# A mixture-of-experts stage: down projection in three reduced passes over split operands, and its weights' order in the queue

## The chip, the cores and the metric

One core of one Trainium2 chip runs the whole program. The metric is the device time in microseconds of one execution; all runs here are on one core.

## The reference

Two transformer stacks are computed one after the other on 256 tokens of 1024 features. The layer that matters here is the feed-forward part of the second layer of the first stack, a mixture of eight experts with two choices for each token:

```python
def moe_swiglu(h, router_w, w1, w3, w2):
    top_v, top_i = lax.top_k(h @ router_w, TOP_K)          # TOP_K = 2, N_EXPERTS = 8
    probs = jax.nn.softmax(top_v, axis=-1)
    gates = jnp.sum(jax.nn.one_hot(top_i, N_EXPERTS) * probs[..., None], axis=-2)
    out = jnp.zeros_like(h)
    for e in range(N_EXPERTS):
        out = out + gates[..., e:e + 1] * swiglu(h, w1[e], w3[e], w2[e])
    return out                                             # swiglu: (silu(h @ w1) * (h @ w3)) @ w2
```

w1 and w3 are 1024x1408 for each expert, w2 is 1408x1024, all in float32. The rest (a hybrid mixer, two more stacks of attention with short convolutions, four more dense feed-forward parts, modulation from a condition) is not touched by the change.

## The kernel before

Matrix products are made in three passes nearly everywhere. A weight `w` is split into a high part, which ScalarE writes as a copy in the reduced 32-bit type F32R, and a low part, the difference, which VectorE writes in the same type. The activations are split likewise, and TensorE adds high times high, low times high and high times low in one PSUM bank. The splits of all weights go through one ring `WS` of three slots: ScalarE may write unit n as soon as TensorE has finished unit n - 3 (`unit_done`, `unit_done >= n - 2`), VectorE follows it (`split_high`), and TensorE follows VectorE (`split_both`).

The expert phase (`experts()` on each engine, `load_experts()` on SyncE) works on 11 blocks of 128 slots. A slot holds one token for one expert, and `BLOCK_EXPERT` says which expert's weights a block needs, so SyncE reads that number and asks for the weights block by block. For each block:

- **up**: 16 units (`UP_UNITS`), two for each of eight k-tiles of 128 rows: even units are w1 rows, odd ones w3 rows, 1408 columns. Raw rows come as k-tiles (w1 and w3 rows together, 2 x 704 KB) into `RAW`, three slots. A unit is nine passes (columns 512, 512, 384). In blocks 0 to 6 small products with `w_ada_2` (`ada_rows`, `ada_turned`) stand between units 1, 6 and 11, and ScalarE asks for the next 1.57 MB of `w_ada_2` when it comes to unit 11 (blocks 0 to 5).
- **turn**: ScalarE takes the silu, VectorE multiplies (three pieces, L2134), TensorE turns the hidden activations in three pieces (L935), ScalarE copies them to `HIDT` (L1583). Between the first and the second piece TensorE scatters the output of the block before to its tokens (L949), and VectorE later adds that to the residual (eight operations, L1956).
- **down**: 11 k-tiles (`GT`) of w2, two products of 128x512 each, on whole float32 operands: raw w2 rows come as pairs of k-tiles (1024 KB, the sixth half as much) into `W2R`, four slots, and TensorE reads them there (L959). In even blocks, behind the sixth k-tile, TensorE gathers the tokens of the next two blocks (`gather`, L879) and their gates (`slot_gates`, L887); VectorE has made the selecting matrices before (`pick`, L2034 and L2035), ScalarE copies the gathered tokens (`block_high`, L1542) and the gates (L1549), and VectorE makes the low parts (`block_low`, L2057). The gather needs the banks of the scatter, so it waits until all eight residual additions are done.
- **output**: ScalarE scales and copies two halves to `YS` (L1598), VectorE makes the low part (L2154) and, ahead of that, the scattering matrix (`place`, L2043 and L2044). The up pass of the next block may run its unit 0 (w1) at once, but unit 1 needs the banks that hold the output, so it waits for `moe_y_split`.

All weights of the phase are asked for on one queue in program order, so a request that waits for its slot holds all behind it. The order for block b is k-tile 0, the last two pairs of block b - 1, k-tiles 1 and 2, pairs 0 and 1, k-tile 3, pair 2, k-tiles 4 and 5, pair 3, k-tiles 6 and 7. A k-tile waits until the k-tile three before it is split; a pair waits until TensorE has multiplied the pair four before it.

## Time and profile before

| | us |
|---|---|
| median of 3 runs | 3255.27 (3250.29 to 3255.81) |
| the profiled execution | 3252.38 |
| its span, first to last instruction | 3250.6 |
| TensorE busy (matmul records) | 3044.6, 94% of the span |
| VectorE busy | 1504.8, 46% |
| ScalarE busy | 1264.3, 39% |
| mean granted TensorE clock | 0.962 of full speed |
| first up unit of block 0 to the end of down of block 10 | 704 to 1362, about a fifth of the span |

A matmul record can overlap the next, so busy TensorE is not TensorE at its peak; the chain of waits shows what released each instruction. A period in this text is the time from the end of the up pass of one block to the end of the up pass of the next; it is even or odd by the block at which it starts. There are ten, from 742.15 to 1340.06.

### The profile page before, as it was taken

The numbers are of one execution on the slowest core, as the hardware profiler recorded it, in microseconds if no ns is written. First come the engines' busy times: TensorE is split into PE (matmuls) and PEld (weight loads), VectorE is DVE, ScalarE is ACT, GpSimd is POOL, SyncE is SP. The second block draws the span as 40 slices with busy tenths as digits, with TensorE's granted clock in tenths as the row PEclk, the third lists the DMA queues.
The fourth block names the chain that finished last, engine by engine and source line by source line (L and its number), as shares of the span: only waits on it lengthen the run. The fifth ranks groups of instructions, "written<-read, shape, count | busy, mean of one in ns | idle before, by whom it ended". The sixth has DMA issues, their size and how long they took to land.

```text
span 3250.6 us, 43934 instructions
## 1 busy us (share of the span) xinstructions
PE 3044.6 (94%) x16943; PEld 2449.5 (75%) x16943; DVE 1504.8 (46%) x2172; ACT 1264.3 (39%) x1789; POOL 0.2 (0%) x4
## 2 busy tenths in 40 slices
PE   6998998989999999789999999999999999989899
PEld 5887887976676666567777777777787777777898
DVE  4553446556566555542323455433334233356555
ACT  4453334444444444342222344432224222245444
POOL 0000000000000000000000000000000000000000
PEclk8999999979999999889999999999999999999899
DMA  8738773367887876636364121443534636422454
GB/s 292 248 114 254 212 241 119 103 232 279 337 338 270 320 300 262 218 112 200 91 173 141 56 85 28 115 149 85 144 102 119 201 96 169 145 69 75 136 168 133
DMA packets 493957, 563.29 MB, mean 173 GB/s; under 512 B 14979, under 2 KB 449734, under 8 KB 493638
## 3 DMA queue, kind: packets, MB, share of 16 engines
q1 hardware_dynamic: 414278, 442.46, 41.2%
q10 hardware_dynamic: 79488, 118.12, 11.4%
q8 instruction: 140, 2.29, 0.3%
q14 instruction: 51, 0.42, 0.0%
HBM read 559.48 MB, written 1.05 MB: 172 GB/s over the span
## 4 chain that ended last, share of the span: by engine, by line
PE 81%; ACT 6%; DMA 6%; DVE 5%; issue 2%; SPq 0%; ACTq 0%; DVEq 0%
PE bank L709 19%; PE bank L711 18%; PE bank L710 18%; PE bank L959 6%; DMA weights_raw<-in_moe_w 4%; PE bank L737 3%; PE bank L908 2%; PE bank L910 2%; PE bank L909 2%; ACT ring L1457 2%; DMA ada_halves<-in_ada_w 1%; DVE weights_split L2048 1%; PE bank L744 1%; PE bank L1355 1%; ACT weights_split L1534 1%
## 5 line engine op out<-in xcount | busy, mean ns | idle before, releaser
L709 PE MATMUL bank<-hn_split,weights_split 128*128 128x256 f32 (+1 forms) x2480 | 875.1, 353 | 68.7 <-DVE hn_split L1938 28.8
L711 PE MATMUL bank<-hn_split,weights_split 128*128 128x256 f32 (+1 forms) x2480 | 849.9, 343 | 2.0 <-issue 2.0
L710 PE MATMUL bank<-hn_split,weights_split 128*128 128x256 f32 (+1 forms) x2480 | 850.5, 343 | 0.0
L1892 DVE TENSOR_TENSOR weights_split<-weights_raw,weights_split 128x1024 fp32r<-128x1024 f32 (+1 forms) x430 | 553.9, 1289 | 248.7 <-ACT weights_split L1403 245.4
L1403 ACT ACTIVATE weights_split<-weights_raw 128x1024 fp32r<-128x1024 f32 (+1 forms) x430 | 475.3, 1107 | 454.6 <-PE bank L711 443.8
L709 PEld LDWEIGHTS bank<-hn_split,weights_split 128*128 128x128 f32 x2480 | 483.7, 195 | 203.3 <-issue 113.1
L711 PEld LDWEIGHTS bank<-hn_split,weights_split 128*128 128x128 f32 x2480 | 483.2, 195 | 52.2
L710 PEld LDWEIGHTS bank<-hn_split,weights_split 128*128 128x128 f32 x2480 | 484.4, 195 | 49.7 <-issue 1.9
L1975 DVE TENSOR_TENSOR ring<-ring,bank 128x512 f32<-128x512 f32 (+1 forms) x110 | 63.9, 581 | 705.7 <-PE bank L711 649.3
L2048 DVE TENSOR_TENSOR weights_split<-weights_raw,weights_split 128x1408 fp32r<-128x1408 f32 x176 | 282.7, 1623 | 180.8 <-ACT weights_split L1534 180.8
L1534 ACT ACTIVATE weights_split<-weights_raw 128x1408 fp32r<-128x1408 f32 x176 | 239.2, 1381 | 194.8 <-DMA weights_raw<-in_moe_w 122.0
L709 PE MATMUL bank<-hidden_split,weights_split 128*128 128x512 f32 (+1 forms) x880 | 308.6, 351 | 0.0
L710 PE MATMUL bank<-hidden_split,weights_split 128*128 128x512 f32 (+1 forms) x880 | 305.1, 347 | 0.0
L711 PE MATMUL bank<-hidden_split,weights_split 128*128 128x512 f32 (+1 forms) x880 | 305.1, 347 | 0.0
L908 PE MATMUL bank<-weights_split,block_split 128*128 128x512 f32 x528 | 210.4, 398 | 23.3 <-DVE weights_split L2048 23.2
L1492 ACT ACTIVATE hidden_split<-ring 128x512 fp32r<-128x512 f32 (+1 forms) x110 | 60.1, 546 | 420.7 <-DVE ring L1975 420.7
L959 PE MATMUL bank<-expert_down,block_hidden_turned 128*128 128x512 f32 x484 | 210.8, 593 | 0.0
L910 PE MATMUL bank<-weights_split,block_split 128*128 128x512 f32 x528 | 201.3, 381 | 0.0
L909 PE MATMUL bank<-weights_split,block_split 128*128 128x512 f32 x528 | 200.0, 379 | 0.0
L709 PEld LDWEIGHTS bank<-hidden_split,weights_split 128*128 128x128 f32 x880 | 166.6, 189 | 32.4 <-issue 11.3
L711 PEld LDWEIGHTS bank<-hidden_split,weights_split 128*128 128x128 f32 x880 | 166.7, 189 | 20.9
L710 PEld LDWEIGHTS bank<-hidden_split,weights_split 128*128 128x128 f32 x880 | 166.7, 189 | 19.8
(362 smaller groups left out, 2964.6 us busy)
## 6 DMA issues: line engine op xcount, KB each, us to landing
weights_raw<-in_moe_w SPq DMA_DIRECT2D x176, 704.0 KB, 7.5
weights_raw<-in_w_ffn_in SPq DMA_DIRECT2D x176, 512.0 KB, 5.1
ada_halves<-in_w_ada ACTq DMA_DIRECT2D x96, 768.0 KB, 5.2
expert_down<-in_moe_w SPq DMA_DIRECT2D x55, 1024.0 KB, 8.9
ada_halves<-in_ada_w ACTq DMA_DIRECT2D x54, 768.0 KB, 4.9
weights_raw<-in_w_in SPq DMA_DIRECT2D x60, 512.0 KB, 4.8
weights_raw<-in_w_ffn_out SPq DMA_DIRECT2D x32, 768.0 KB, 4.7
weights_raw<-in_ffn_w SPq DMA_DIRECT2D x44, 512.0 KB, 5.4
```

Of the source, the lines that this page charges most:

```text
L709: mm(ps, wh, xh, start=first, stop=False)
L710: mm(ps, wh, xl, start=False, stop=False)
L711: return mm(ps, wl, xh, start=False, stop=last)
L737: i = mm(PS[bank][32 * j:32 * j + 32, 0:ADA_COLS], condp[:, 4 * h + j, :], AH[:, h, j, :], start=h == 0, stop=h == 1)
L908: mm(ps, xh, wh, start=k == 0, stop=False)
L909: mm(ps, xl, wh, start=False, stop=False)
L910: i = mm(ps, xh, wl, start=False, stop=k == KT - 1)
L959: i = mm(PS[4 + h][:, :], HIDT[:, f, :], W2R[:, m % W2_PAIRS, f % 2, h * 512:(h + 1) * 512], start=f == 0, stop=f == GT - 1)
L1403: act.activation(split_view(slot, 0, kts, n), raw, ACT.Copy).then_inc(split_high, 1)
L1534: act.activation(up_split(n, 0), up_raw(n), ACT.Copy).then_inc(split_high, 1)
L1892: tt(split_view(slot, 1, kts, n), raw, split_view(slot, 0, kts, n).bitcast(F32), ALU.subtract)\
L2048: tt(up_split(n, 1), up_raw(n), up_split(n, 0).bitcast(F32), ALU.subtract).then_inc(split_both, 1)
```

## The change

The down projection is made in three passes like the others. w2's k-tiles become units 16 to 26 of each block in the ring of splits (`BLOCK_UNITS` = 27), so ScalarE and VectorE split them as they do the up units. `HIDT` gets a high and a low part, the low one made by VectorE (`hidden_low`) from the bank that ScalarE copied. The six passes of a k-tile replace two whole products. `W2R` has three slots in place of four, and a pair waits until the pair three before it is split. SyncE's order for block b becomes: k-tiles 0, 1 and 2, then pairs 3, 4 and 5 of block b - 1, then k-tile 3, pair 0, k-tile 4, pair 1, k-tile 5, pair 2, k-tiles 6 and 7. The programs of ScalarE and VectorE in `experts()` are reordered: the splits of w2's later k-tiles stand among VectorE's residual additions, ScalarE's copies of the gather stand behind the copy of unit 23, and the splits of units 0 and 1 of the next block stand ahead of the placing and the output, that of unit 2 behind them. The wait for all splits at the end of `load_experts` now includes w2's. The diff, without lines that only rename or count semaphores:

```diff
+BLOCK_UNITS = UP_UNITS + GT
 UP_CHUNKS = ((0, 512), (512, 512), (1024, 384))
-W2_PAIRS = 4
+W2_PAIRS = 3
...
-        HIDT, _ = at("block_hidden_turned", FFN_GROUP, [P, GT, P], F32, g_at + W2_PAIRS * 2 * D + FFN_GROUP)
+        HIDT, _ = at("block_hidden_turned", 2 * FFN_GROUP, [P, 2, GT, P], F32R, g_at + W2_PAIRS * 2 * D + FFN_GROUP)
...
                     kk = KT * b + k
-                    sp.wait_ge(split_both, MOE_U + 2 * max(0, kk - 2))
+                    sp.wait_ge(split_both, MOE_U + ((kk - 3) // KT * BLOCK_UNITS + 2 * ((kk - 3) % KT) + 2 if kk >= 3 else 0))
...
                         m = n - W2_PAIRS
-                        sp.wait_ge(S["moe_down"], GT * (m // DOWN_PAIRS) + min(2 * (m % DOWN_PAIRS) + 2, GT))
+                        sp.wait_ge(split_both, MOE_U + m // DOWN_PAIRS * BLOCK_UNITS + UP_UNITS + min(2 * (m % DOWN_PAIRS) + 2, GT))
...
                     expert[b] = sp.value_load(BLOCK_EXPERT[0:1, b:b + 1], min_val=0, max_val=EXPERTS - 1)
-                    up_tile(b, 0)
+                    for k in range(3):
+                        up_tile(b, k)
                     if b:
-                        down_pair(b - 1, 4)
-                        down_pair(b - 1, 5)
-                    up_tile(b, 1)
-                    up_tile(b, 2)
-                    down_pair(b, 0)
-                    down_pair(b, 1)
-                    up_tile(b, 3)
-                    down_pair(b, 2)
-                    up_tile(b, 4)
-                    up_tile(b, 5)
-                    down_pair(b, 3)
+                        for q in range(3, DOWN_PAIRS):
+                            down_pair(b - 1, q)
+                    for k in range(3, 6):
+                        up_tile(b, k)
+                        down_pair(b, k - 3)
                     up_tile(b, 6)
                     up_tile(b, 7)
-                down_pair(MOE_BLOCKS - 1, 4)
-                down_pair(MOE_BLOCKS - 1, 5)
-                sp.wait_ge(split_both, MOE_U + UP_UNITS * MOE_BLOCKS)
+                for q in range(3, DOWN_PAIRS):
+                    down_pair(MOE_BLOCKS - 1, q)
+                sp.wait_ge(split_both, MOE_U + BLOCK_UNITS * MOE_BLOCKS)
...
 
                 def down(b):
                     for f in range(GT):
-                        pe.wait_ge(S["moe_hidden_copied"], 3 * b + f // 4 + 1)
-                        m = DOWN_PAIRS * b + f // 2
-                        pe.wait_ge(wide_full[m % W2_PAIRS], 16 * (m // W2_PAIRS + 2))
+                        n = BLOCK_UNITS * b + UP_UNITS + f
+                        pe.wait_ge(S["moe_hidden_split"], 3 * b + f // 4 + 1)
+                        pe.wait_ge(split_both, MOE_U + n + 1)
+                        hh, hl = (HIDT[:, part, f, :] for part in (0, 1))
                         for h in range(2):
-                            i = mm(PS[4 + h][:, :], HIDT[:, f, :], W2R[:, m % W2_PAIRS, f % 2, h * 512:(h + 1) * 512],
-                                   start=f == 0, stop=f == GT - 1)
+                            wh, wl = (expert_split(n, part)[:, h * 512:(h + 1) * 512] for part in (0, 1))
+                            mm(PS[4 + h][:, :], hh, wh, start=f == 0, stop=False)
+                            mm(PS[4 + h][:, :], hl, wh, start=False, stop=False)
+                            i = mm(PS[4 + h][:, :], hh, wl, start=False, stop=f == GT - 1)
                             if h:
-                                i.then_inc(S["moe_down"], 1)
+                                i.then_inc(unit_done, 1)
...
-                def split_up(n):
-                    block = MOE_B + n // 2
-                    act.wait_ge(raw_full[block % 3], 32 * (block // 3 + 1))
+                def split_expert(n):
+                    b, v = n // BLOCK_UNITS, n % BLOCK_UNITS
+                    if v < UP_UNITS:
+                        block = MOE_B + KT * b + v // 2
+                        act.wait_ge(raw_full[block % 3], 32 * (block // 3 + 1))
+                    else:
+                        m = DOWN_PAIRS * b + (v - UP_UNITS) // 2
+                        act.wait_ge(wide_full[m % W2_PAIRS], 16 * (m // W2_PAIRS + 2))
                     act.wait_ge(unit_done, MOE_U + n - 2)
-                    act.activation(up_split(n, 0), up_raw(n), ACT.Copy).then_inc(split_high, 1)
+                    act.activation(expert_split(n, 0), expert_raw(n), ACT.Copy).then_inc(split_high, 1)
...
                 table(ACT.Silu)
                 block_high(0, 1)
                 for n in range(3):
-                    split_up(n)
+                    split_expert(n)
                 slot_gates(0, 1)
+                last = BLOCK_UNITS * MOE_BLOCKS
                 for b in range(MOE_BLOCKS):
-                    for v in range(3, UP_UNITS):
+                    n = BLOCK_UNITS * b
+                    for v in range(3, UP_UNITS + 1):
                         if v == 11 and b + 1 < x.n_turns:
                             copy_ada(b + 1)
-                        split_up(UP_UNITS * b + v)
-                    act.wait_ge(unit_done, MOE_U + UP_UNITS * b + UP_UNITS - 1)
+                        split_expert(n + v)
+                    act.wait_ge(unit_done, MOE_U + n + UP_UNITS - 1)
                     for c, (c0, cn) in enumerate(UP_CHUNKS):
                         act.activation(HID[:, c0:c0 + cn], PS[c][:, 0:cn], ACT.Silu).then_inc(S["moe_silu"], 1)
+                    split_expert(n + UP_UNITS + 1)
                     for c, (c0, cn) in enumerate(UP_CHUNKS):
                         act.wait_ge(S["moe_hidden_turned"], 3 * b + c + 1)
-                        act.activation(HIDT[:, 4 * c:4 * c + cn // P, :].rearrange("p a b -> p (a b)"),
+                        act.activation(HIDT[:, 0, 4 * c:4 * c + cn // P, :].rearrange("p a b -> p (a b)"),
                                        PS[7 if c == 1 else 6][:, 0:cn], ACT.Copy).then_inc(S["moe_hidden_copied"], 1)
-                    if b + 1 < MOE_BLOCKS:
-                        split_up(UP_UNITS * (b + 1))
-                    if b + 1 < MOE_BLOCKS:
-                        if b % 2 == 0:
+                        if c == 0:
+                            split_expert(n + UP_UNITS + 2)
+                    for v in range(UP_UNITS + 3, BLOCK_UNITS + 1):
+                        if n + v < last:
+                            split_expert(n + v)
+                        if v == UP_UNITS + 7 and b % 2 == 0 and b + 1 < MOE_BLOCKS:
                             block_high(b + 1, 2)
                             slot_gates(b + 1, 2)
-                        split_up(UP_UNITS * (b + 1) + 1)
-                        split_up(UP_UNITS * (b + 1) + 2)
+                    if b + 1 < MOE_BLOCKS:
+                        split_expert(n + BLOCK_UNITS + 1)
                     act.wait_ge(S["moe_gate_copied"], (b + 1) // 2 + 1)
                     if b:
                         act.wait_ge(S["moe_scattered"], 4 * b)
                     for h in range(2):
-                        act.wait_ge(*((S["moe_down"], GT * (b + 1)) if h else (S["moe_y_part"], b + 1)))
+                        act.wait_ge(*((unit_done, MOE_U + BLOCK_UNITS * (b + 1)) if h else (S["moe_y_part"], b + 1)))
                         act.activation(YS[:, 0, h * 512:(h + 1) * 512], PS[4 + h][:, :], ACT.Copy,
                                        scale=SLOT_GATE[:, b % 4:b % 4 + 1]).then_inc(S["moe_y_high"], 1)
+                    if b + 1 < MOE_BLOCKS:
+                        split_expert(n + BLOCK_UNITS + 2)
                 u0 = next_split[0] = PH["ffna.0"][0]
...
+                def split_expert(n):
                     dve.wait_ge(split_high, MOE_U + n + 1)
-                    tt(up_split(n, 1), up_raw(n), up_split(n, 0).bitcast(F32), ALU.subtract).then_inc(split_both, 1)
+                    tt(expert_split(n, 1), expert_raw(n), expert_split(n, 0).bitcast(F32), ALU.subtract).then_inc(split_both, 1)
+
+                def hidden_low(b, c):
+                    dve.wait_ge(S["moe_hidden_copied"], 3 * b + c + 1)
+                    cn = UP_CHUNKS[c][1]
+                    hh, hl = (HIDT[:, part, 4 * c:4 * c + cn // P, :].rearrange("p a b -> p (a b)") for part in (0, 1))
+                    tt(hl, PS[7 if c == 1 else 6][:, 0:cn], hh.bitcast(F32), ALU.subtract).then_inc(S["moe_hidden_split"], 1)
...
 
                 for b in range(MOE_BLOCKS):
-                    for v in range(3, UP_UNITS):
-                        split_up(UP_UNITS * b + v)
+                    n = BLOCK_UNITS * b
+                    for v in range(3, UP_UNITS + 1):
+                        split_expert(n + v)
                     if b + 1 < x.n_turns:
                         add_modulation(b + 1)
                     for c, (c0, cn) in enumerate(UP_CHUNKS):
                         dve.wait_ge(S["moe_silu"], 3 * b + c + 1)
-                        dve.wait_ge(*((S["moe_up_part"], 2 * b + c + 1) if c < 2 else (unit_done, MOE_U + UP_UNITS * (b + 1))))
+                        dve.wait_ge(*((S["moe_up_part"], 2 * b + c + 1) if c < 2 else (unit_done, MOE_U + n + UP_UNITS)))
                         tt(HID[:, c0:c0 + cn], HID[:, c0:c0 + cn], PS[3 + c][:, 0:cn], ALU.mult).then_inc(S["moe_hidden"], 1)
+                    split_expert(n + UP_UNITS + 1)
+                    hidden_low(b, 0)
+                    split_expert(n + UP_UNITS + 2)
+                    hidden_low(b, 1)
+                    hidden_low(b, 2)
                     if b + 1 < MOE_BLOCKS and b % 2 == 0:
                         pick(b + 1, 0, 2)
                         pick(b + 2, 1, 2)
-                    if b:
-                        for k in range(KT):
-                            dve.wait_ge(S["moe_scattered"], 4 * (b - 1) + k // 2 + 1)
-                            residual(k, 0, PS[(2, 3, 0, 1)[k // 2]][:, k % 2 * SEQ:(k % 2 + 1) * SEQ], gate(k),
+                    for v in range(UP_UNITS + 3, BLOCK_UNITS):
+                        split_expert(n + v)
+                        q = v - UP_UNITS - 3
+                        for k in (2 * q, 2 * q + 1) if b and q < 4 else ():
+                            dve.wait_ge(S["moe_scattered"], 4 * (b - 1) + q + 1)
+                            residual(k, 0, PS[(2, 3, 0, 1)[q]][:, k % 2 * SEQ:(k % 2 + 1) * SEQ], gate(k),
                                      x0 + KT * (b - 2) + k + 1 if b > 1 else None)
                     if b + 1 < MOE_BLOCKS:
-                        split_up(UP_UNITS * (b + 1))
                         if b % 2 == 0:
                             block_low(b + 1, 2)
-                        split_up(UP_UNITS * (b + 1) + 1)
-                        split_up(UP_UNITS * (b + 1) + 2)
+                        split_expert(n + BLOCK_UNITS)
+                        split_expert(n + BLOCK_UNITS + 1)
                     place(b)
                     dve.wait_ge(S["moe_gate_copied"], (b + 1) // 2 + 1)
                     for h in range(2):
...
                             ALU.mult, ALU.subtract).then_inc(S["moe_y_split"], 1)
+                    if b + 1 < MOE_BLOCKS:
+                        split_expert(n + BLOCK_UNITS + 2)
                 u0 = next_split[0] = PH["ffna.0"][0]
```

## Rows read from the trace of the kernel before

**Rows 1.** The page's costliest groups, down's matmuls: busy us, mean ns.

```profile
L959 PE MATMUL bank<-expert_down,block_hidden_turned 128*128 128x512 f32 x484 | 210.8, 593 | 0.0
```

**Rows 2.** Windows, even periods summed, then odd: length, busy, PEclk, DMA share, GB/s.

```profile
sum 306.50, PE 297.54 PEld 215.00 DVE 186.62 ACT 143.76 POOL 0.00; mean PE 59.51 PEld 43.00 DVE 37.32 ACT 28.75 POOL 0.00
...
1161.81:1219.95 58.14, 55.03 (x217) 38.73 (x214) 32.57 (x32) 25.94 (x24) 0.00 (x0) 0.97 0.74 298
1281.41:1340.06 58.65, 54.35 (x217) 38.63 (x215) 32.86 (x32) 26.05 (x24) 0.00 (x0) 0.97 0.68 271
sum 291.41, PE 278.09 PEld 194.98 DVE 164.59 ACT 131.12 POOL 0.00; mean PE 55.62 PEld 39.00 DVE 32.92 ACT 26.22 POOL 0.00
```

**Rows 3.** Chain of waits in two periods: start us, us, what.

```profile
1164.93 18.89 PE bank L959 x44
1183.81 0.23 PE bank L908
...
1233.56 3.83 PE bank L879 x32
...
1246.88 0.23 PE bank L908
```

**Rows 4.** Timeline of ScalarE: start us, us, engine, line, operation, idle before it.

```profile
974.54 2.65 ACT L1534 ACTIVATE weights_split<-weights_raw 128x1408 fp32r<-128x1408 f32 x2 [2.02 <-DMA weights_raw<-in_moe_w]
...
1187.75 1.38 ACT L1534 ACTIVATE weights_split<-weights_raw 128x1408 fp32r<-128x1408 f32 x1 [0.54 <-PE bank L910]
1189.67 1.38 ACT L1534 ACTIVATE weights_split<-weights_raw 128x1408 fp32r<-128x1408 f32 x1 [0.53 <-PE bank L910]
...
1207.37 2.65 ACT L1534 ACTIVATE weights_split<-weights_raw 128x1408 fp32r<-128x1408 f32 x2 [3.23 <-DMA weights_raw<-in_moe_w]
1210.83 1.38 ACT L1534 ACTIVATE weights_split<-weights_raw 128x1408 fp32r<-128x1408 f32 x1 [0.82 <-DMA weights_raw<-in_moe_w]
```

**Rows 5.** Timeline of TensorE, the first pass of unit 12.

```profile
1210.46 0.50 PE L908 MATMUL bank<-weights_split,block_split 128*128 128x512 f32 x1 [1.78 <-DVE weights_split L2048]
```

**Rows 6.** Windows of one period, columns as in rows 2.

```profile
1157.00:1169.00 12.00, 12.00 (x60) 9.02 (x60) 9.04 (x15) 6.11 (x9) 0.00 (x0) 1.00 0.01 2
...
1175.00:1211.00 36.00, 32.89 (x131) 23.83 (x130) 20.50 (x16) 17.77 (x15) 0.00 (x0) 1.00 1.02 414
1211.00:1214.00 3.00, 3.00 (x9) 2.58 (x8) 2.57 (x2) 1.21 (x1) 0.00 (x0) 0.50 0.59 242
```

**Rows 7.** Timeline of SyncE's queue, down's fifth and sixth pair asked for.

```profile
930.07 3.77 SPq L649 DMA_DIRECT2D expert_down<-in_moe_w  x2
...
1168.53 3.77 SPq L649 DMA_DIRECT2D expert_down<-in_moe_w  x2
```

**Rows 8.** Timeline of all engines, the first two splits after the expert phase.

```profile
1362.84 2.00 ACT L1403 ACTIVATE weights_split<-weights_raw 128x1024 fp32r<-128x1024 f32 x2
...
1363.92 2.36 DVE L1892 TENSOR_TENSOR weights_split<-weights_raw,weights_split 128x1024 fp32r<-128x1024 f32 x2 [0.19 <-ACT weights_split L1403]
```

**Rows 9.** Timeline of VectorE, odd period.

```profile
1160.69 1.85 DVE L2134 TENSOR_TENSOR block_hidden<-block_hidden,bank 128x512 f32<-128x512 f32 x3 [1.50 <-PE bank L910]
...
1183.87 1.46 DVE L2154 SCALAR_TENSOR_TENSOR block_out_split<-bank,small,block_out_split 128x512 fp32r<-128x512 f32 x2 [1.02 <-ACT block_out_split L1598]
```

**Rows 10.** Timeline of VectorE, even period.

```profile
1220.86 0.28 DVE L2034 TENSOR_SCALAR block_pick<-route_tables,small 128x128 fp32r<-128x128 f32 x1
...
1223.19 3.22 DVE L1956 SCALAR_TENSOR_TENSOR residual<-bank,mod_first,residual 128x256 f32<-128x256 f32 x8
...
1236.21 1.42 DVE L2057 TENSOR_TENSOR block_split<-bank,block_split 128x256 fp32r<-128x256 f32 x4 [8.27 <-ACT block_split L1542]
```

**Rows 11.** Timeline of ScalarE, even period, the last copy of the gates.

```profile
1238.51 0.27 ACT L1549 ACTIVATE small<-bank 128x1 f32<-128x1 f32 x2
```

**Rows 12.** The tile of w_ada, two loads of two halves each.

```profile
DMA to landing us min/median/max: 12.5/14.2/16.5
```

**Rows 13.** Timeline of VectorE after the last block, its first residual.

```profile
1366.20 0.87 DVE L1956 SCALAR_TENSOR_TENSOR residual<-bank,mod_first,residual 128x256 f32<-128x256 f32 x2
```

32 lines of the change are left out of this document (17 added, 15 removed).

## The prediction

> **What bounds the kernel now.** I first read the page, to see what the diff touches: the matmuls of down, 484 records for 242 instructions, are 210.8 us of TensorE, all in the expert phase [rows 1]. So I cut that phase into periods, each from the end of one block's up pass to the end of the next one's. The ten periods fall into two kinds [rows 2]: five that start at an even block take 306.5 us (61.3 each), five that start at an odd one 291.4 us (58.3 each). In the even ones TensorE also gathers the tokens of the next two blocks. The reader should see in the sums that VectorE is busy for only 186.6 and 164.6 us of them, so its total is no limit.
>
> The chain of waits shows what a period is made of [rows 3]. Below, t counts from the end of the up pass. Odd: turning and scattering until 3.1, 44 records of down for 18.89 us, next up pass from 1183.81, t = 22.0. Even: the same with the gather (3.83) and the gates in between, next up pass from 1246.88, t = 26.9. An up unit takes 1.92 us [rows 4], so 16 take 30.7; the pass that starts at 1183.81 ends at 1219.95, after 36.1. The 5.4 us too many are transfers: ScalarE stands waiting for k-tiles 6 and 7 of w1 and w3 [rows 4]. k-tile 6 lands at 1207.37, unit 12 starts at 1210.46 after 1.78 us of idle TensorE [rows 5], 3.09 later (one split on each engine), and four units more would end the pass at 1218.1. The other 1.8 us are the clock: the granted clock reads 0.50, the lower of the two levels, from 1211 to 1214 [rows 6].
>
> Why are the tiles late? From 1157 to 1169 nothing moves (2 GB/s), from 1175 on 414 GB/s for 36 us [rows 6]. The queue is in order, and it stands at the fifth pair of w2, which waits for the second k-tile of down; it is issued at 1168.53 [rows 7]. So the period is idle queue, then a burst, then four last units.
>
> **The change, part by part.** *TensorE.* A pass over 512 columns takes 512/1408 of a third of 1.92 us, 0.232; six of them make a k-tile of down 1.39 us, eleven 15.3, where 44 matmuls of the old kind take 18.89. Unhidden, this would give 3.6 us a block.
>
> *The splits.* Per block eleven copies on ScalarE and eleven subtractions on VectorE, 128x1024: two in a row take 2.00 and 2.36 us [rows 8], so 1.0 and 1.15 us each. VectorE gets 12.7 us a block, and 1.75 more for the low half of the activations (no row shows this operation; 1408 columns of a PSUM product take 1.85 [rows 9], four of 256 columns 1.42 [rows 10]; I take the rate of the first, the second would give 1.95). Both total busy times stay far under the period. But they fall into the down stage, behind one another in program order, so I lay out that stage.
>
> *Odd block.* VectorE ends the last hidden product at t = 0.73 (1162.54) [rows 9], splits k-tile f1 until 1.9, halves the first third of the activations until 2.55, f2 until 3.7, the other thirds until 4.85. TensorE starts f0 at 3.1 as before. Slots of the split ring come free only three units later, so f3's copy waits for f0 (4.5): its split ends at 6.85. Now two residual additions (0.40 each, eight in 3.22 us [rows 10]) follow each of f3 to f6: splits end at 6.85, 8.85, 10.8, 12.75, then 14.7, 15.85, 17.0 and 18.5 for f10. TensorE follows them and ends down at 20.3, where before it was 22.0: 1.7 of the 3.6 us are left. Then come the splits of up units 0 and 1 (1.54 each in a row) until 22.2, the placing (0.75, estimated from two operations of 256 columns) and the halving of the output (1.46 [rows 9]) until 24.4. Before, the placing and both splits lay earlier, in idle time. Unit 1 needs the output's banks, so it starts at 24.45, against 22.0 + 1.92 = 23.9.
>
> *Even block.* The eight pick operations (1220.86 until the first residual at 1223.19, 2.4 us with the overlap [rows 10]) come ahead of f3. Splits then end at 8.4, 10.35, 12.3 and 14.25, the last residual at 15.05. The gather waits for all residuals, so it starts at 15.05 although f5 ends at 13.8. ScalarE's copy for f8 stands behind the copies of the gather in its program; those end 5.2 us after the gather starts (1233.56 to 1238.78 [rows 3, 11]), at 20.3. So f8's split ends at 22.5, f9's 23.65, f10's 24.8; then block_low (twice 1.42) until 27.6, unit 0's split 29.15, unit 1's 30.7, placing and output until 32.95. Up starts at 29.2 and its unit 1 at 33.0; before 26.9 and 28.85. Block 0 has no residuals: 28.0 in place of 30.7.
>
> *The queue.* The k-tiles 0 to 2 of the next block are now asked for as units 11, 13 and 15 are split, and the last pairs as down is split. All of that lands within the first 14 us. But k-tile 3 still waits for the split of unit 1, R = 22.2 (odd), 30.7 (even), 28.0 (block 0), and the first pair of w2 stands behind it. The idle stretch is not gone, it has moved, and more must come after it: five k-tiles of 2 x 704 KB and three pairs of 1024 KB, 10.4 MB (the shapes in the code). At 414 GB/s [rows 6], with 1.5 us of start that I estimate from the time between the issue at 1168.53 and the rise to that rate (bounds 0 and 4), k-tile 6 lands at R + 23.0, k-tile 7 at R + 26.5. By the 3.05 us of two splits and four units this ends the pass at R + 33.75. From unit 1 on TensorE alone would end at R + 2.25 + 28.8 = R + 31.05, so transfers stay last.
>
> In the up passes of blocks 1 to 5, 1.57 MB of w_ada are loaded too, from about R + 17. They took 14.2 us to land [rows 12], about 0.27 of the rate: up to 3.3 us for k-tile 7; the kernel before needs 44.5 us from the first request to that tile with them (930.07 to 974.54 [rows 7, 4]) and 42.3 without (1168.53 to 1210.83): 2.2. I take 2.5, so k-tile 7 lands at R + 29.0 and the pass ends at R + 35.9. (The Trainium skill, "DMA: Bandwidth & Descriptors", section "Queues, rings and completion order", has each DMA engine go round its queues packet by packet, which would give w_ada up to half of the engines. Its whole 1.57 MB would then be ahead of k-tile 7, 3.8 us for 2.5, and five such periods would make the sum 6.5 us higher; the 14.2 us of the row speak for a smaller share.)
>
> *Ends.* In the first up pass one pair less is ahead of k-tile 7 (1 MB, 2.5 us at 414 GB/s), and the queue stands idle once more, since k-tile 3 must wait for unit 1's split and no second pair fills that time: 0, with 2.5 us of gain as the bound. After the last block down ends 1.7 us earlier, but ffna's first weights are now asked for after the last split (t = 18.6; before, right behind the last pair), land near 23.5 (1 MB, for which I estimate 5 us with the start), and both engines split two units of them before the residuals (2.00 and 2.36 us, the second 1.2 us behind the first): these start near 27.0, before at 1366.20 - 1340.06 = 26.1 [rows 2, 13]. +0.9.
>
> *Sum.* Even periods: 63.9 + 2 x 66.6 + 2 x 64.45 = 326.0 against 306.5, +19.5. Odd: 2 x 58.1 + 3 x 55.95 = 284.05 against 291.4, -7.4. With +0.9: +13.0. The span becomes 3263.6. The profiled execution took 3252.4 for a span of 3250.6 and the median of the runs is 3255.3, so I add the 13 to that: 3268 us.
>
> **Rivals.** *1. Transfers no longer bind (faster).* If k-tile 6 lands before R + 20.3, TensorE's own time holds: odd 53.25, even 61.8 (block 0: 59.1), and 1.9 more (one unit, an estimate) where w_ada is multiplied in. That makes 270.1 and 312.0 us, with the end -15: 3240 us. For it: three k-tiles are ready early. Against: 8.9 MB after R at 414 GB/s. It decides at some 475 GB/s, which no window that I read reaches. A cheaper way to the same side: vector splits that run ahead so that the even handover costs 3 us less in five periods, -15: 3253. Chance of ending below -0.2%: 0.2.
>
> *2. The splits and the moved requests cancel.* Each even period 2 to 4 us shorter than laid out, because a wait that I put in series overlaps: 3250 to 3261 us. 0.2.
>
> *3. As forecast*, 3262 to 3275 us: 0.4.
>
> *4. The clock also falls.* Now the periods from 1161.81 and 1281.41 read 0.97 [rows 2], as do two others of the ten. The new down stage has TensorE idle for about 0.5 to 1 us ahead of most k-tiles and 2.5 us ahead of the even up pass. One fall costs 1.8 us where nothing covers it; in all ten periods 18: 3286 us. 0.2. (The Trainium skill, "TensorE: Matmul & The Clock Gate", section "HAM oscillation", describes just this, a clock that falls again at each wait for a transfer; the trace so far shows it in under half of the periods.)
>
> Range: rival 1 below, rival 4 above, 3238 to 3290. A difference under 0.2% (6.5 us) can't be told from none here. Chances from the cases: faster 0.2, same 0.2, slower 0.6; the likeliest case alone 3262 to 3275.
>
> **What would show it.** Right: down stages of about 20.3 us to its end in odd blocks, 26.7 in even; up starting at 20.7 and 29.2; a wait before up unit 1 on the output's halving; the queue empty from t = 14 to R; ScalarE waiting for k-tiles 5 to 7; even periods longer by 3 to 5 us and odd ones shorter by 1 to 2. Wrong: no wait for transfers in up (rival 1), even handovers below 27 us (rival 2), or a clock of 0.97 in most periods (rival 4). What would upset the whole is a VectorE whose splits take another time than 1.15 us, since the even handover adds some sixteen of its operations in series.

## The result and the profile after

| | before | after |
|---|---|---|
| median, us (5 runs each) | 3252.2 (3247.06 to 3255.81) | 3288.87 (3286.66 to 3293.43) |
| ratio | | 1.0111, interval 1.0099 to 1.0123 |
| span of the profiled execution | 3250.6 | 3284.9 |
| mean granted clock | 0.962 | 0.962 |

The change makes the kernel 36.7 us slower, where 13 were forecast. The page of the kernel after, busy time and the chain's shares by engine and by line:

```profile
PE 3023.5 (92%) x17185; PEld 2489.5 (76%) x17185; DVE 1659.6 (51%) x2326; ACT 1388.8 (42%) x1910; POOL 0.2 (0%) x4
...
PE 75%; DVE 10%; ACT 7%; DMA 6%; issue 3%; SPq 1%; ACTq 0%; DVEq 0%
PE bank L709 19%; PE bank L711 18%; PE bank L710 18%; DVE weights_split L2063 4%; DMA weights_raw<-in_moe_w 4%; PE bank L737 3%; PE bank L908 2%; PE bank L910 2%; PE bank L909 2%; ACT weights_split L1542 2%; ACT ring L1460 1%; DMA ada_halves<-in_ada_w 1%; DVE residual L1971 1%; PE bank L744 1%; PE bank L1358 1%
```

VectorE has 155 us more work and is still at 51% of the span; TensorE has 21 us less. Nothing here says slower. The periods do. Windows over the even ones (the first and the last of five), then over the odd ones (the fourth of five), each with its sum (columns as in [rows 2]):

```profile
740.05:807.03 66.98, 59.06 (x285) 47.56 (x284) 49.04 (x55) 40.15 (x47) 0.00 (x0) 0.95 0.74 290
...
1251.93:1318.42 66.49, 56.17 (x279) 45.94 (x277) 51.66 (x62) 39.67 (x46) 0.00 (x0) 1.00 0.69 260
sum 337.85, PE 295.50 PEld 239.59 DVE 256.37 ACT 199.94 POOL 0.00; mean PE 59.10 PEld 47.92 DVE 51.27 ACT 39.99 POOL 0.00
...
1193.48:1251.93 58.45, 52.90 (x239) 42.35 (x237) 46.91 (x46) 37.24 (x36) 0.00 (x0) 0.97 0.77 298
...
sum 298.96, PE 269.78 PEld 213.83 DVE 235.25 ACT 187.62 POOL 0.00; mean PE 53.96 PEld 42.77 DVE 47.05 ACT 37.52 POOL 0.00
```

Against the sums of [rows 2] the even periods are 31.35 us longer and the odd ones 7.55, together 38.9. The prediction had 19.5 and -7.4. The rest of the 34.3 us between the spans: the first period starts 2.1 us earlier (740.05 for 742.15), since its up pass began 3.2 us earlier, at 701.80 for 704.97, and took 1.2 us longer; the first residual behind the last block comes at 1406.40, t = 29.5, for 26.1 [rows 2, 13], so +3.4; and from there to the end, in code that the change doesn't touch, this execution took 5.9 us less (1878.5 for 1884.4).

**The handover.** The chain of waits in the odd period from 1193.48 and the even one from 1251.93 (start us, us, what), where [rows 3] had one unbroken down:

```profile
1198.27 1.07 ACT weights_split L1542
...
1204.34 0.87 DVE residual L1971 x2
1205.21 1.13 DVE weights_split L2063
1206.35 0.79 DVE residual L1971 x2
1207.13 1.14 DVE weights_split L2063
...
1212.93 3.16 DVE weights_split L2063 x2
1216.10 0.28 DVE first_choice_place L2058
1216.43 0.37 issue
1216.80 1.41 DVE block_out_split L2182 x2
1218.25 0.50 PE bank L908
...
1265.98 0.80 DVE residual L1971 x2
1266.83 4.10 PE bank L879 x32
...
1277.01 2.65 DVE block_split L2078 x8
1279.66 3.07 DVE weights_split L2063 x2
1282.73 0.28 DVE first_choice_place L2058
1283.06 0.37 issue
1283.43 1.41 DVE block_out_split L2182 x2
1284.89 0.51 PE bank L908
```

VectorE's program order is the chain from the third k-tile of down to the next block's unit 1. By t: R, the end of unit 1's split, is 22.6 (1216.09), unit 1 at 24.8 (1218.25); in the even period the gather starts at 14.9, R is 30.8 (1282.73), unit 1 is at 33.0. The forecast was 22.2, 24.45, 15.05, 30.7, 33.0.

**The up pass.** ScalarE's timeline, in which it waits for k-tiles 4 to 7 in turn (k-tile 7 is the line of the single split), and SyncE's queue, which asks for k-tile 3 right after R:

```profile
1229.07 2.65 ACT L1542 ACTIVATE weights_split<-weights_raw 128x1408 fp32r<-128x1408 f32 x2 [1.39 <-DMA weights_raw<-in_moe_w]
1235.07 2.65 ACT L1542 ACTIVATE weights_split<-weights_raw 128x1408 fp32r<-128x1408 f32 x2 [3.35 <-DMA weights_raw<-in_moe_w]
1241.06 2.65 ACT L1542 ACTIVATE weights_split<-weights_raw 128x1408 fp32r<-128x1408 f32 x2 [3.34 <-DMA weights_raw<-in_moe_w]
1244.52 1.38 ACT L1542 ACTIVATE weights_split<-weights_raw 128x1408 fp32r<-128x1408 f32 x1 [0.81 <-DMA weights_raw<-in_moe_w]
```

```profile
1195.67 9.26 SPq L654 DMA_DIRECT2D expert_down<-in_moe_w  x3
1216.25 0.35 SPq L644 DMA_DIRECT2D weights_raw<-in_moe_w  x1
```

k-tile 6 lands at R + 25.0 and k-tile 7 at R + 28.4, where 23.0 and 26.5 were forecast, and the pass ends at R + 35.8 for 33.75. Windows of the same stretch (last column GB/s) show the start of the burst in halves of a microsecond, then its steady rate:

```profile
1216.50:1217.00 0.50, 0.35 (x2) 0.03 (x1) 0.50 (x2) 0.23 (x2) 0.00 (x0) 1.00 0.00 0
1217.00:1217.50 0.50, 0.00 (x0) 0.00 (x0) 0.50 (x2) 0.50 (x1) 0.00 (x0) 1.00 0.69 123
1217.50:1218.00 0.50, 0.00 (x0) 0.00 (x0) 0.50 (x2) 0.50 (x1) 0.00 (x0) 1.00 0.81 203
1218.00:1218.50 0.50, 0.25 (x1) 0.25 (x2) 0.50 (x2) 0.32 (x1) 0.00 (x0) 1.00 0.70 248
1218.50:1219.00 0.50, 0.50 (x3) 0.41 (x3) 0.50 (x1) 0.00 (x0) 0.00 (x0) 1.00 1.02 406
...
1219.00:1237.00 18.00, 17.05 (x79) 14.11 (x78) 12.45 (x9) 10.12 (x8) 0.00 (x0) 1.00 1.02 414
```

The rate is the 414 GB/s of [rows 6]. 10.36 MB at that rate are 25.0 us; k-tile 7 took 28.4. So 3.4 us come on top, not 1.5. A window from R to the landing of k-tile 7 shows where the rest is:

```profile
1216.09:1244.50 28.41, 24.55 (x106) 19.96 (x105) 20.00 (x17) 15.45 (x12) 0.00 (x0) 0.94 0.97 389
```

389 GB/s over 28.41 us are 11.05 MB, 0.69 more than the tiles up to k-tile 7 hold. So about 1.7 us are lost before the rate is up, and another 1.7 lie between the last bytes of k-tile 7 and the landing that ScalarE sees, in which bytes of later requests move already.

**The clock.** The last 8 us of the up passes of blocks 4, 6, 7 and 8, in windows (the clock is the third number from the end):

```profile
989.69:997.69 8.00, 8.00 (x32) 6.79 (x31) 5.56 (x7) 5.54 (x7) 0.00 (x0) 0.80 1.03 403
1119.30:1127.30 8.00, 8.00 (x33) 6.86 (x31) 5.66 (x7) 4.59 (x7) 0.00 (x0) 0.80 0.79 277
1185.48:1193.48 8.00, 7.77 (x36) 6.67 (x37) 7.10 (x7) 5.55 (x7) 0.00 (x0) 1.00 0.97 357
1243.93:1251.93 8.00, 7.78 (x37) 6.68 (x37) 7.09 (x7) 5.55 (x7) 0.00 (x0) 1.00 0.92 335
```

The passes of blocks 1 to 6 all read 0.80 to 0.87 there, those of 7 to 10 all 1.00 (that of block 0, with w_ada's products too, also 1.00). From k-tile 6's landing to the end of the pass the six take 12.42 us and the four 10.87. In the kernel before, a pass with the products of `ada_rows` takes 11.68 at full clock. So of those 1.55 us about 0.8 are the products and 0.7 the clock. The kernel before had four such falls (0.84 to 0.89). Three were in passes without these products, blocks 8 to 10, where the same stretch took 12.2 to 12.6 us, and 10.87 is the time at full clock: 1.3 to 1.7 us each. So the clock took no less from the kernel before than from the one after. In block 8 the clock falls too (0.77 from 1237 to 1240, 0.66 to 1243), but earlier, mostly under the wait for k-tile 6.

### The profile page after: what moved, and what is told of

It is laid out like the page before. It is cut to its first block, busy times and chain, and to the rows that moved or that the text cites. A ratio compares the mean times of both kernels' runs of the same rounds, so it can differ in the third digit from the quotient of the medians.

```text
span 3284.9 us, 44814 instructions
## 1 busy us (share of the span) xinstructions
PE 3023.5 (92%) x17185; PEld 2489.5 (76%) x17185; DVE 1659.6 (51%) x2326; ACT 1388.8 (42%) x1910; POOL 0.2 (0%) x4
## 4 chain that ended last, share of the span: by engine, by line
PE 75%; DVE 10%; ACT 7%; DMA 6%; issue 3%; SPq 1%; ACTq 0%; DVEq 0%
PE bank L709 19%; PE bank L711 18%; PE bank L710 18%; DVE weights_split L2063 4%; DMA weights_raw<-in_moe_w 4%; PE bank L737 3%; PE bank L908 2%; PE bank L910 2%; PE bank L909 2%; ACT weights_split L1542 2%; ACT ring L1460 1%; DMA ada_halves<-in_ada_w 1%; DVE residual L1971 1%; PE bank L744 1%; PE bank L1358 1%
## 5 line engine op out<-in xcount | busy, mean ns | idle before, releaser
L908 PE MATMUL bank<-weights_split,block_split 128*128 128x512 f32 x528 | 213.0, 403 | 54.5 <-DVE weights_split L2063 44.6
L910 PE MATMUL bank<-weights_split,block_split 128*128 128x512 f32 x528 | 205.4, 389 | 0.0
L909 PE MATMUL bank<-weights_split,block_split 128*128 128x512 f32 x528 | 204.5, 387 | 0.0
L1492 ACT ACTIVATE ring<-bank 128x512 f32<-128x512 f32 (+1 forms) x110 | 56.3, 512 | 314.3 <-PE bank L711 314.2
```

The lines of the kernel that those rows point to most:

```text
L908: mm(ps, xh, wh, start=k == 0, stop=False)
L909: mm(ps, xl, wh, start=False, stop=False)
L910: i = mm(ps, xh, wl, start=False, stop=k == KT - 1)
```

## Experiments

Below, "up" is the time from the first up unit to the end of the pass, "hand" from the end of the pass to the next first unit. Hand and up, read from each trace's TensorE timeline, are (even / odd, block 0's left out; for up, first the passes of blocks 7 to 10, then those of blocks 1 to 6, which hold w_ada's products). The last column is the time from the end of the first up pass to that of the last:

In the old down the first matmul record of an up pass starts some 0.5 us before down's last product has ended, so its hand is short by that. The start of unit 1 is the same thing in both kernels: it comes 2.32 us after the pass's first record in the old down and 3.55 in the new one (2.76 in e7, e9 and e10).

| kernel | ratio to before, interval | hand | up | all ten periods |
|---|---|---|---|---|
| before | 1 | 26.3 / 21.6 | 34.9 to 37.2, 35.0 to 37.5 | 597.9 |
| after | 1.0111 (1.0099, 1.0123) | 29.4 / 21.2 | 36.8 to 37.2, 39.2 to 40.1 | 636.8 |
| e1 | 1.0012 (1.0003, 1.0022) | 29.4 / 21.2 | 33.2 to 34.7, 35.1 to 36.4 | 600.9 |
| e2 | 0.9981 (0.9970, 0.9992) | 26.3 / 21.6 | 34.4 to 36.7, 34.8 to 36.3 | 594.7 |
| e3 | 1.0064 (1.0044, 1.0084) | 29.4 / 21.2 | 35.7 to 37.7, 35.4 to 39.1 | 624.6 |
| e4 | 0.9995 (0.9982, 1.0009) | 29.4 / 21.2 | 32.8 to 34.8, 35.1 to 36.0 | 597.1 |
| e5 | 0.9898 (0.9875, 0.9921) | 26.3 / 21.6 | 31.1 to 31.5, 33.7 to 33.9 | 566.3 |
| e6 | 0.9943 (0.9922, 0.9964) | 26.3 / 21.6 | 32.5 to 33.7, 34.1 to 35.3 | 580.5 |
| e7 | 0.9960 (0.9944, 0.9975) | 26.4 / 21.4 | 32.8 to 35.4, 34.3 to 35.7 | 582.9 |
| e8 | 0.9946 (0.9930, 0.9962) | 26.7 / 18.8 to 19.9 | 33.3 to 34.6, 35.1 to 38.4 | 583.4 |
| e9 | 0.9907 (0.9890, 0.9924) | 26.4 / 21.4 | 31.6 to 31.7, 34.2 to 34.3 | 570.0 |
| e10 | 0.9922 (0.9905, 0.9938) | 26.4 / 21.4 | 31.6 to 32.2, 34.2 to 34.3 | 570.3 |
| e11 | 0.9896 (0.9880, 0.9913) | 26.3 / 21.6 | 31.4 to 32.5, 33.7 | 569.4 |

### Which half of the change costs: e1, e2, e3

**e1**, after, with the pairs ahead of k-tile 3:

```diff
-                    for k in range(3, 6):
+                    for q in range(3):
+                        down_pair(b, q)
+                    for k in range(3, KT):
                         up_tile(b, k)
-                        down_pair(b, k - 3)
-                    up_tile(b, 6)
-                    up_tile(b, 7)
```

> The changed kernel with one edit: the queue asks for pairs 0, 1 and 2 of a block ahead of its k-tile 3, so that 3.1 MB move while the queue now stands empty (t = 14 to R, where R is the end of unit 1's split). Theory A (the up pass ends when 10.4 MB after R have landed, with 3.4 us of start and landing on top of 414 GB/s, then 3.05 us of splits and two units): only 7.2 MB are left after R, k-tile 7 lands at R + 20.8, before TensorE wants it (R + 24.2), so a period becomes R + 31.05, about 1.9 more with w_ada, 5 us less than now in each of ten: 3289 - 52 = 3237 us. Theory B (the late handover by VectorE and ScalarE sets the pass, and its waits for tiles only mirror it): no change, 3285 to 3293.

Measured: 3256.46 us. The order of the queue alone is worth 32 us of the changed kernel, nearly as much as its whole loss against before, but not the 52 that were expected. Handovers are as in after, to 0.1 us.

**e2**, before, with the next block's k-tiles 0 to 2 asked for first:

```diff
-                    up_tile(b, 0)
+                    for k in range(3):
+                        up_tile(b, k)
                     if b:
                         down_pair(b - 1, 4)
                         down_pair(b - 1, 5)
-                    up_tile(b, 1)
-                    up_tile(b, 2)
```

> The kernel before with only the order of requests changed: k-tiles 0, 1 and 2 of a block ahead of the last two pairs of the block before, then pairs 0 and 1, k-tile 3 and the rest as before; down stays two whole float32 products for each k-tile. Theory A: from the split of unit 1 on (t = 20.2 odd, 23.2 even) 9.3 MB are left, k-tile 7 lands at t = 46.1 and 49.1, the pass would end at 53 and 56, TensorE's own work at 52.7 and 57.6 (1.9 more with w_ada); ten periods 566 in place of 598: 3252 - 32 = 3220 us. Theory B: transfers do not set it, 3245 to 3255.

Measured: 3246.8 us, a gain of 6 us for an expected 32. SyncE's queue and the rates, in one up pass of e2:

```profile
1193.48 0.33 SPq L639 DMA_DIRECT2D weights_raw<-in_moe_w  x1
1193.90 0.38 SPq L640 DMA_DIRECT2D weights_raw<-in_moe_w  x1
1194.47 0.38 SPq L649 DMA_DIRECT2D expert_down<-in_moe_w  x1
1197.32 0.34 SPq L639 DMA_DIRECT2D weights_raw<-in_moe_w  x1
```

```profile
1183.00:1188.00 5.00, 5.00 (x22) 3.76 (x21) 1.60 (x3) 2.76 (x3) 0.00 (x0) 1.00 1.02 421
1188.00:1197.00 9.00, 9.00 (x44) 7.73 (x43) 7.85 (x5) 6.51 (x5) 0.00 (x0) 1.00 0.86 308
```

The requests come 3.84 us apart, as units are split, and the queue runs at 308 GB/s in a stretch where it had room for 414. A k-tile may be asked for only when the one three before it is split, so there is a round from a freed slot to its next contents that the bytes over the rate don't show. That this round was the cause is at this point argued only; e10 and e11 test it.

**e3**, after, with the order of before: k-tile 0, pairs 3 to 5 of the block before, k-tiles 1 and 2, pair 0, k-tile 3, pair 1, k-tiles 4 and 5, pair 2, k-tiles 6 and 7.

> The changed kernel with requests as near to the old order as three slots of w2 allow: k-tile 0, pairs 3 to 5 of the block before, k-tiles 1 and 2, pair 0, k-tile 3, pair 1, k-tiles 4 and 5, pair 2, k-tiles 6 and 7. Theory A: pair 0 has landed before R, so 9.3 MB are left in place of 10.4, k-tile 7 lands 2.5 us earlier in each period: 3264 us. If asking ahead for the k-tiles is what helps the changed kernel (rival), undoing it makes this one slower than 3289. Theory B: no change.

Measured: 3273.64 us, where 3264 were expected. Of the changed kernel's loss 15 us are the new order against the old one (4.8 in the even periods, 7.6 in the odd ones); e1's order is worth 17 more.

### What the new down costs with fewer bytes: e4, e5, e8

**e4** is after and **e5** before, each with a quarter of w3:

```diff
-                    sp.dma_start(RAW[:, s, FFN_GROUP:], a["moe_w3"][0][expert[b]][r, :]).then_inc(raw_full[s], 16)
+                    sp.dma_start(RAW[:, s, FFN_GROUP:FFN_GROUP + 352], a["moe_w3"][0][expert[b]][r, 0:352]).then_inc(raw_full[s], 16)
```

> The changed kernel with only 352 of the 1408 columns of w3 loaded (the rest of the tile keeps what stood there, so part of the up product is left out); order, waits and all work on the engines stay. A k-tile is 0.90 MB in place of 1.44. Theory A: 7.7 MB after R land by R + 21.9, TensorE's own pace holds, period R + 31.05: about 3237 us, as with the pairs first. Theory B: no change, 3285 to 3293.

> The kernel before with only 352 of the 1408 columns of w3 loaded (part of the up product is left out), the partner of the changed kernel with fewer bytes, which took 0.9995 of the kernel before. Here no transfer should bind in either, so the two show what the new down stage costs by itself. Theory A (the handover of the new down stage is longer than the old one: even 29.4 against 26.3 us and unit 1 another 2 us later, odd 21.2 against 21.6 and unit 1 0.5 us later): up passes of 30.7 us (32.8 with w_ada), ten periods 559, 39 us under the kernel before: 3213 us, 37 below its partner. Rival C (three passes are cheaper than whole products as soon as transfers don't bind): this one at or above its partner's 3250.

Measured: 3250.3 us for the 3237 expected, and 3217.77 for 3213. With few bytes the new down still costs 32.5 us. Four even handovers are 3.0 us longer, the first 2.1, five odd ones 0.4 shorter (+12.2); and unit 1 of each block starts 3.55 us after unit 0 in place of 2.32, by the output's low part behind both splits and the placing (+12.3 in ten blocks). The two make 24.4 of the 30.8 us between the ten periods of e4 and e5. The other 6.3 lie between unit 1 and the end of the pass, and are transfers: e4 keeps the changed kernel's order of requests, and ScalarE still waits for k-tiles in it, between 740 and 1309 (us in total, times, longest):

```profile
ACT weights_split L1542 <- DMA weights_raw<-in_moe_w: 22.5, 18, 2.6
```

The same cut fits the full kernels. Of the 38.9 us that the change adds to the ten periods, 24.6 are the later start of unit 1 and the rest the stretch from unit 1 to the end of the pass. e1 leaves the starts of unit 1 where they are in the changed kernel and takes its 36 us from that stretch alone. So its order of requests makes up for the late handover; it doesn't show that the order was the whole cause of the loss.

**e8** is e1 with VectorE's low part made for half of the columns of w2:

```diff
-                    tt(expert_split(n, 1), expert_raw(n), expert_split(n, 0).bitcast(F32), ALU.subtract).then_inc(split_both, 1)
+                    c = slice(0, FFN_GROUP if n % BLOCK_UNITS < UP_UNITS else 512)
+                    tt(expert_split(n, 1)[:, c], expert_raw(n)[:, c], expert_split(n, 0)[:, c].bitcast(F32),
+                       ALU.subtract).then_inc(split_both, 1)
```

> The changed kernel with the pairs first, and VectorE making the low part of only 512 of the 1024 columns of each k-tile of w2 (the other half of the low part is left out). An operation of 1.14 us becomes 0.6. Theory A: odd handovers from 21.2 to about 18.9 us, even ones from 29.4 to about 26.1, 28 us if the tiles are there: 3228 us. If VectorE isn't what sets the down stage, handovers stay at 21.2 and 29.4 and the time at 3256.

Measured: 3232.74 us, 24 less than e1, of which 17.5 lie in the ten periods and the rest behind them; handovers are 2.7 us shorter in even and 1.3 to 2.4 in odd blocks. So VectorE paces the down stage, although it is half idle over the span. It is also why three passes don't shorten the odd handover: it is 21.2 us for 21.6 before, where TensorE's share of it fell by an estimated 3.6.

### Mending the handover and the queue: e6, e7, e9, e10, e11

**e6** is e2 with pairs 2 and 3 both ahead of k-tile 4.

> The old down with the new queue, and pairs 2 and 3 both ahead of k-tile 4. With pair 3 between k-tiles 5 and 6, k-tile 6 took 10.7 us from request to landing, and the transfer engines ran at 265 to 355 GB/s between 1188 and 1197, since each k-tile may be asked for only when the one three before is split. Theory D (three raw slots and what stands between their requests set the up pass): pair 3 fills that dip, k-tiles 6 and 7 land 2.5 us earlier in each of ten periods: 3247 - 25 = 3222 us. Theory E (total bytes at 414 GB/s set it): no change, 3242 to 3252.

Measured: 3233.52 us, faster than both kernels, and about half of the 25 us that theory D gave.

**e7** is e1 with ScalarE's `block_high` behind the copy for f8 (f0 to f10 are down's k-tiles), the residual additions done with f5, the placing behind `hidden_low` (odd) or f7 (even), and `block_low` behind f8:

```diff
-                        if v == UP_UNITS + 7 and b % 2 == 0 and b + 1 < MOE_BLOCKS:
+                        if v == UP_UNITS + 8 and b % 2 == 0 and b + 1 < MOE_BLOCKS:
...
-                        for k in (2 * q, 2 * q + 1) if b and q < 4 else ():
+                        for k in ((0, 1), (2, 3, 4), (5, 6, 7))[q] if b and q < 3 else ():
...
```

> The changed kernel with the pairs first, and three moves in the programs of ScalarE and VectorE: ScalarE's copy for k-tile f8 ahead of the copies of the gather; VectorE's placing in its idle time (odd: ahead of f3; even: behind f7), its residuals done with f5, and block_low behind f8 in place of behind f10. Theory A (the handover is a chain through VectorE's and ScalarE's program order): even handover 29.4 to about 26 us and unit 1 from 33.0 to 29.0, odd unit 1 0.75 us earlier; 24 us in all if the tiles are there: 3256 - 24 = 3232 us. Rival (the slots of raw tiles take it back, since the requests then come no faster in up): 3245 to 3256.

Measured: 3237.76 us, 18.7 less than e1. The even handover is back at 26.4, and unit 1 comes 2.76 us after unit 0, not 3.55. No work was removed, so this part of the cost was order. Not all of it came through: ScalarE's waits for k-tiles between 740 and 1309 grew from 26.9 us in e1 to 48.1.

**e9** is e7 with e4's fewer bytes.

> The kernel of e7 (the changed kernel with pairs 0 to 2 asked for ahead of k-tile 3 and with the handover's steps reordered), and only 352 of the 1,408 columns of w3 are loaded in each k-tile, so the units of w3 are worked out from what else lies in the slot. It asks whether the 32.5 us that the new down pass costs with few bytes (e4, 3250, against e5, 3218) is all order of steps at the handover. If it is, the two fixes add in full: hand-overs of 26.4 and 21.4 us as in e7, up passes of 31 to 32 us and 33.7 with w_ada as in e5, and 3218 to 3222 us. If part of it is the work itself (the low part of w2 on VectorE, 11 more subtractions of 1,024 columns in each block, or the whole product), the up pass or the first units of a block stay later than in e5, as in e4 (32.8 to 33.6), and the time is 3231 (e4 less the 18.7 us that e7 gained over e1).

Measured: 3220.57 us. Against e5's 3217.77 the new down's 32.5 us are gone but for 3, and the intervals of the two ratios overlap, so even these are not clear of noise; in the two traces the ten periods differ by 3.7 us, all of it the later unit 1. Two things differ between e4 and e9, the handover's steps and the pairs asked for first. Of the 27 us between their ten periods 20.7 are the earlier unit 1, so the order of steps at the handover, and 6.5 the waits for k-tiles, of which e9 has none. What is left of the new down's cost, with all low parts of w2 made, is these 3 us.

**e10** is e7, each half of a k-tile asked for by itself:

```diff
-                    sp.wait_ge(split_both, MOE_U + ((kk - 3) // KT * BLOCK_UNITS + 2 * ((kk - 3) % KT) + 2 if kk >= 3 else 0))
+                    freed = MOE_U + (kk - 3) // KT * BLOCK_UNITS + 2 * ((kk - 3) % KT) if kk >= 3 else MOE_U - 2
                     r, s = slice(k * P, (k + 1) * P), (MOE_B + kk) % 3
+                    sp.wait_ge(split_both, freed + (1 if kk >= 3 else 2))
                     sp.dma_start(RAW[:, s, 0:FFN_GROUP], a["moe_w1"][0][expert[b]][r, :]).then_inc(raw_full[s], 16)
+                    sp.wait_ge(split_both, freed + 2)
                     sp.dma_start(RAW[:, s, FFN_GROUP:], a["moe_w3"][0][expert[b]][r, :]).then_inc(raw_full[s], 16)
```

> The kernel of e7, and SP asks for the w1 half of a k-tile as soon as the w1 unit of the k-tile three before is split, and for its w3 half when that one's w3 unit is split; until now both waited for the second. If the up pass is held by the round from a freed slot to its next contents (e7's ScalarE waits 22.9 us for k-tiles in four blocks, up passes 33 to 35.5 us against 31 to 31.5 with few bytes), the first halves set out some 2 us sooner and about half of this wait goes: up passes 32 to 34 us, 3218 to 3228 us. If the rate of the queue holds it (the bytes of a block over 414 GB/s), the requests only queue up earlier: up passes as before, 3236 to 3240 us.

Measured: 3224.27 us, with all bytes loaded. Its up passes are those of e9. ScalarE's waits for k-tiles between 740 and 1309 (us in total, times, longest), in e7 and then in e10:

```profile
ACT weights_split L1541 <- DMA weights_raw<-in_moe_w: 48.1, 34, 3.1
```

```profile
ACT weights_split L1543 <- DMA weights_raw<-in_moe_w: 3.6, 4, 1.4
```

The same bytes on the same queue, each w1 half asked for 1.4 to 1.8 us sooner than its w3 half, hardly bind any more. So what held the up passes of e7 was the round from a freed slot to its contents and not the queue's rate.

**e11** is e6 with the same split of the request, on the old down: the control for e10.

> The kernel before (down as two whole products) in e6's order of requests, and each half of a k-tile is asked for when the unit that frees its place is split, as in e10. It is the control for e10: is the new down pass worth anything once the queue and the handover are mended? If the round from a freed slot to its contents is all that holds e6's up passes (33 to 35.3 us against 31.1 to 33.8 in e5), they fall to e5's and the time is 3218 to 3222 us, so that the new down pass costs some 3 us even in its best version here. If the old order, in which pairs 0 to 3 of w2 need all four slots, keeps a transfer in the way, the gain is half of that or less, 3226 to 3233 us, and e10 stays the fastest.

Measured: 3220.64 us. The waits for k-tiles in the same stretch:

```profile
ACT weights_split L1534 <- DMA weights_raw<-in_moe_w: 17.2, 15, 2.3
```

The intervals of e10 and e11 overlap, so which is faster isn't settled; the three-pass down is not the faster one in any pair that was measured. The gain of e10 over before is in the order and the timing of the requests, since e11 has it without the new down.

## Why the prediction was right in sign and too small

The forecast was 13 us slower, the measured change 36.7. The periods came out 26.8 us longer than laid out (636.8 for 610.05). In parts:

- **Handover, right.** R was 0.4 late in the odd periods and the first, 0.1 in the other even ones: 2.8 us in all. The laid-out order (copy for f8 behind the gather's copies, output behind both splits and the placing) is in the chain as written. Unit 1 starts 0.8 us later than before in odd periods and 4.3 in most even ones, 24.6 us in ten. Two readings were a little off and changed nothing: the low half of the activations was put at 1.75 us where the row that it goes by gives 1.85, and up unit 1 of before was put at t = 28.85 in even periods, where the trace has 28.7.
- **The step that failed: the queue, "with 1.5 us of start".** The mechanism held (queue empty until R, k-tile 3 asked for at R, burst at 414 GB/s, k-tiles 4 to 7 late), but the term was mis-sized. k-tile 6 landed at R + 25.0, not 23.0. The passes of blocks 7 to 10 end 1.9 us late for it, and ten times that is 19.4 of the 26.8. The value was taken from the time until the rate rises; what counts is the time from request to landing over the bytes by the rate. [Rows 4, 7] had it: 42.3 us for 15.9 MB, which at 414 GB/s are 38.3, so 4.0 on top. Some 0.8 of these are a dip of the queue between two pairs of w2 (256 GB/s from 1172 to 1174), which the burst behind R doesn't have.
- **w_ada, a little low and short by one pass.** k-tile 7 landed at R + 30.1 to 30.9 with the load, where 29.0 was forecast; after the 1.9 above, the load itself cost 1.7 to 2.5 for the 2.5 taken. The pass of block 6 was laid out without w_ada, since nothing is loaded there. Its products are still in it, and with the clock it ended at R + 37.8 for 33.75. These six passes hold the other 4.5 us.
- **w_ada's share of the transfers.** k-tile 7 came 1.7 to 2.5 us later in the passes with the load than in block 8's without (R + 28.4). The prediction's estimate by the Trainium skill, "DMA: Bandwidth & Descriptors", "Queues, rings and completion order", was 3.8 us; the measured delay lies around the 2.2 that [rows 4, 7] gave, and under the 3.3 from [rows 12]. No run here took w_ada away.
- **Rival 4, the clock, was partly true and did not decide.** The last 8 us of six passes were granted 0.80 to 0.87, about 0.7 us each, so some 4 us where 18 were allowed. Four passes of before had it too (0.84 to 0.89) and paid no less for it, and the mean of the span is 0.962 in both. That the measured 3289 is near this rival's 3286, and inside the range whose upper end it set, is luck: its mechanism gave a quarter of what it allowed. In block 8's pass the fall (0.77 and 0.66 between 1237 and 1243) lay mostly under the wait for k-tile 6. That agrees with the Trainium skill, "TensorE: Matmul & The Clock Gate", "HAM oscillation", on when the clock falls; its price is what the wait doesn't cover.
- **Rival 1, right about where the gain is.** Its 3240 was for the changed kernel with its own handover. e4 comes nearest to that, 3250 us with some waits for k-tiles left. With the old down or the handover mended too, the time drops to 3218 to 3224 (e5, e9, e10, e11). That this takes some 475 GB/s was wrong: e10 loads all bytes at 323 GB/s on average (750 to 1050), and requests made sooner did it.
- **Rival 2, cancelling,** is refuted: the even handover is 29.4 us, as laid out.
- **Ends.** The first pass took 1.2 us longer, where 0 was taken and up to 2.5 of gain allowed; that it ended 2.1 us earlier comes from its earlier start, in code that the change doesn't touch. The tail was +3.4 for +0.9: ffna's first weights, asked for at 1396.16, were split from 1403.03, so 6.9 us for the 5 estimated, the queue's term once more. By the spans the miss is 21.3 us (34.3 for 13.0): 26.8 of the periods and 2.5 of the tail, less the 2.1 by which the first pass ended earlier and the 5.9 that the untouched rest took less.

My own expectations behind the prediction failed in one way five times: e1, e2, e3, e4 and e6 were each given the whole of the transfers' wait and returned a fifth to three quarters of it. The reason, that a bound by bytes over rate leaves the slots out, is shown by e10 and e11 for the orders of e7 and e6, and argued only for the others.

What stays open: what sets the 1.7 us between the last bytes and the landing, whether w_ada's share of the transfers is what its load costs, and whether e10 or e11 is the faster.

## What to carry to other kernels

Size a late transfer by a row from its request to its landing of the same burst, not by bytes over the steady rate. When weights come through a few slots, look at how early each request may go out: splitting the request so that each half follows its own slot's release gave about 13 us in two kernels, with no byte less. And before moving work to a half-idle engine, write out its program order across the handover: what stands behind the moved work, and who waits for that, was most of the price, 20.7 of the 27 us between e4 and e9.

## What was not expected of the hardware

- A burst on an empty queue: 0 GB/s until 0.75 us after the request, 123 to 248 for 1.5 us, then 414 on average. Over 10.4 MB the last tile lands 3.4 us later than the bytes at 414 GB/s, half of it before the rate is up and half behind the last bytes.
- Three reduced passes over 128x512 are issued 0.23 us apart each, 0.70 in all, against 0.86 for a whole product in two records (18.89 us over 22 in [rows 3]). The gain is 19%. A k-tile costs 1.22 us of VectorE and 1.06 of ScalarE for it, and by e8 it was VectorE that paced the down stage.
- VectorE's operations in a row each hide some 0.1 us of the next: 3.48 us for three splits of 1.22.
